# Transformer layer pair in fp32 on one core: the first attention's scores from stacked high and low parts, and an earlier start of the first norm's squares

## The reference, cut to what matters

```python
def forgetting_attention(q, k, v, log_f):
    # q, k, v: (B, S, H, 64); log_f: log forget gates
    c = jnp.cumsum(log_f, axis=1)
    ...
        s = jnp.einsum('bqhd,bkhd->bhqk', q_i, k) * 64 ** -0.5
        bias = c_i[..., :, None] - c_keys[..., None, :]
        mask = k_pos[None, :] <= q_pos[:, None]
        s = jnp.where(mask, s + bias, NEG_INF)
        p = jax.nn.softmax(s, axis=-1)
        return jnp.einsum('bhqk,bkhd->bqhd', p, v)

xn = rms_norm(h, norm_mix_g)
qa, ka, va, fa, cq, ckv, kr, ga, gb = jnp.split(xn @ w_in, splits)
ya = forgetting_attention(qa, ka, va, log_sigmoid(fa + b_forget))
yb = latent_attention(...)       # 8 heads, query and key of 64 + 32 features
merged = sigmoid(ga) * (ya @ w_branch_a) + sigmoid(gb) * (yb @ w_branch_b)
```

## Time and profile before

| | us |
|---|---|
| median of 3 runs (lowest, highest) | 2146.44 (2146.40, 2148.82) |
| the profiled execution, its own time | 2147.04 |
| its span, from the first to the last instruction | 2145.2 |
| busy: PE, its weight loads, DVE, ACT, POOL | 2110.5, 1784.4, 1324.4, 1007.1, 701.9 |
| mean granted TensorE clock | 0.993 |
| first attention, from head 0's first transpose to head 7's end | 123.2 to 215.1 |

### The profile page before, as it was taken

How to read it: one execution, slowest core, us unless ns; L and a number is a source line. 1 busy time by engine, 2 the same in 40 slices (tenths; PEclk the granted TensorE clock), 3 DMA queues, 4 the chain that set the end, 5 groups by cost and what they waited for, 6 DMA issues and landing times.

```text
span 2145.2 us, 31345 instructions
## 1 busy us (share of the span) xinstructions
PE 2110.5 (98%) x10842; PEld 1784.4 (83%) x10842; DVE 1324.4 (62%) x2182; ACT 1007.1 (47%) x1771; POOL 701.9 (33%) x523
## 2 busy tenths in 40 slices
PE   8999999999999999999999999999999999999998
PEld 6878888888888888898887788888877888888886
DVE  5467774466762276775268788788768336676523
ACT  4345664543442253444234567777646325334322
POOL 2011345323233261443327701211155415133331
PEclk9999999999999999999999999999999999999998
DMA  5211235334433333443234322222264533434321
GB/s 171 79 47 67 84 112 190 101 122 153 150 124 108 98 108 113 161 138 123 94 101 156 118 69 75 79 75 79 94 202 138 185 99 118 135 132 167 104 93 65
DMA packets 73423, 248.15 MB, mean 116 GB/s; under 512 B 8080, under 2 KB 8336, under 8 KB 72944
## 3 DMA queue, kind: packets, MB, share of 16 engines
q1 hardware_dynamic: 51120, 182.08, 26.0%
q0 software_dynamic: 10496, 37.56, 5.1%
q10 hardware_dynamic: 11712, 27.27, 3.5%
HBM read 227.48 MB, written 18.87 MB: 115 GB/s over the span
## 4 chain that ended last, share of the span: by engine, by line
PE 83%; DVE 8%; ACT 2%; POOL 2%; issue 2%; DMA 1%; DVEq 0%; POOLq 0%; SPq 0%; ACTq 0%
PE bank L188 24%; PE bank L190 24%; PE bank L189 24%; PE bank L194 3%; PE bank L195 3%; POOL hid L738 2%; PE bank L2128 2%; DVE w_lo L162 1%; DMA w_raw<-stream 1%; DVE gn_r L2730 1%; PE bank L912 1%; DVE xn_lo L608 1%; ACT w_hi L157 1%; DVE h L622 1%; POOL hid L1471 1%
## 5 line engine op out<-in xcount | busy, mean ns | idle before, releaser
L162 DVE TENSOR_TENSOR w_lo<-w_raw,w_hi 128x1024 fp32r<-128x1024 f32 x337 | 454.8, 1353 | 425.1 <-ACT w_hi L157 422.2
L188 PE MATMUL bank<-xn_hi,w_hi 128*128 128x512 f32 (+1 forms) x1432 | 554.7, 387 | 4.1 <-DVE w_lo L162 2.6
L157 ACT ACTIVATE w_hi<-w_raw 128x1024 fp32r<-128x1024 f32 x337 | 354.7, 1054 | 414.0 <-PE bank L190 248.2
L189 PE MATMUL bank<-xn_lo,w_hi 128*128 128x512 f32 (+1 forms) x1432 | 539.1, 376 | 0.0
L190 PE MATMUL bank<-xn_hi,w_lo 128*128 128x512 f32 (+1 forms) x1432 | 538.8, 376 | 0.0
L188 PEld LDWEIGHTS bank<-xn_hi,w_hi 128*128 128x128 f32 x1432 | 271.1, 189 | 56.6 <-DVE h L622 5.2
L190 PEld LDWEIGHTS bank<-xn_hi,w_lo 128*128 128x128 f32 x1432 | 269.8, 188 | 50.2
L189 PEld LDWEIGHTS bank<-xn_lo,w_hi 128*128 128x128 f32 x1432 | 271.0, 189 | 45.7 <-issue 2.9
L188 PE MATMUL bank<-down_hi,w_hi 128*128 128x512 f32 x528 | 205.8, 390 | 0.0
L190 PE MATMUL bank<-down_hi,w_lo 128*128 128x512 f32 x528 | 205.4, 389 | 0.0
L189 PE MATMUL bank<-down_lo,w_hi 128*128 128x512 f32 x528 | 205.4, 389 | 0.0
(11 more groups left out here) (462 smaller groups left out, 4272.7 us busy)
## 6 DMA issues: line engine op xcount, KB each, us to landing
w_raw<-stream SPq DMA_DIRECT2D x337, 512.0 KB, 3.5
s_raw<-stream POOLq DMA_DIRECT2D x48, 512.0 KB, 6.3
spill_g<-gate_out ACTq DMA_DIRECT2D x16, 256.0 KB, 2.0
m_more<-spill_g POOLq DMA_DIRECT2D x3, 1024.0 KB, 12.5
x<-xt SPq DMA_DIRECT2D x4, 512.0 KB, 7.1
x<-xt ACTq DMA_DIRECT2D x1, 2048.0 KB, 9.3
spill_x<-x ACTq DMA_DIRECT2D x1, 2048.0 KB, 6.5
spill_ga<-ga_out ACTq DMA_DIRECT2D x8, 256.0 KB, 2.1
```

The costliest lines, as they stand in the source:

```text
L157: nc.scalar.activation(w_hi[:, slot, :], w_raw[:, slot % 2, :], ACT.Copy).then_inc(split_hi, 1)
L162: nc.vector.tensor_tensor(w_lo[:, slot, :], w_raw[:, slot % 2, :], w_hi[:, slot, :], ALU.subtract).then_inc(split_lo, 1)
L188: nc.tensor.matmul(to, a_hi, b_hi, start=start, stop=False, skip_group_check=True)
L189: nc.tensor.matmul(to, a_hi, b_lo, start=False, stop=False, skip_group_check=True)
```

## The change

Three things are done.

First, a head's operands are stacked. `q_both` holds the head's query in its high part on the head's own 64 partitions and in its low part on the other 64. `k_own` (two tiles, for even and odd heads) holds the key's high part on the head's own 64 partitions and zeros, set once, on the others. `k_mixed` holds the key's low part on the own 64 and its high part on the others. `q_both` against `k_own` and against `k_mixed`, both on 128 partitions, add up to the three products of before. The triangle product stays. [...] 

Second, head 0's scores are made within the last chunk of V instead of after it, and head 1 is staged ahead of the V staging.

Third, ACT squares tiles 0 to 3 of x ahead of the third chunk's high part, and the fourth chunk's high part comes after the square of tile 5 instead of tile 3.

The diff, with its unchanged lines cut:

```diff
@@ -823,6 +823,9 @@
         ks_hi = sb("ks_hi", [P, S], F32R, W0 + 2 * T2)
...
         vs = sb("vs", [P, TB, 2, P], F32R, W0 + 4 * T2)
+        q_both, k_mixed, k_own = qs_hi, ks_lo, (ks_hi, qs_lo)
+        q_rest = sb("q_rest", [P, S], F32R, 54 * K)
+        crossed = sem("att_crossed")
         prob = sb("prob", [P, 2, OFF[TB]], F32, W0 + 6 * T2)
...
         pt_lo = sb("pt_lo", [P, OFF[TB]], F32R, W0 + 27 * K)
@@ -884,7 +887,7 @@
 
...
             s, z = att_sems, dict(atts)
-            for k, n in dict(staged_hi=16 if latent else 8, staged_lo=16 if latent else 8, v_hi=4, v_lo=4, scored=32,
+            for k, n in dict(staged_hi=16 if latent else 24, staged_lo=16, v_hi=4, v_lo=4, scored=32,
                              biased=32, negated=8, exp=32, inverse=8, scaled=32, turned=32, hi=32, lo=32, summed=32, half=8, out=8,
...
                 atts[k] += n
@@ -892,13 +895,17 @@
             gate0 = 8 if latent else 0
...
             def score(pe, h):
-                r = slice(0, P) if latent else slice(64 * (h % 2), 64 * (h % 2) + 64)
-                pe.wait_ge(s["staged_lo"], 2 * (h + 1 if latent else h // 2 + 1) + z["staged_lo"])
+                pe.wait_ge(s["staged_lo"], 2 * (h + 1) + z["staged_lo"])
+                if not latent:
+                    pe.wait_ge(s["staged_hi"], 3 * (h + 1) + z["staged_hi"])
+                    pe.wait_ge(crossed, 16 * (h + 1))
                 for place_of, qb in enumerate(SCORE_ORDER):
...
                     at, n = slice(qb * P, (qb + 1) * P), (qb + 1) * P
-                    last = mm3(score_bank(qb), qs_hi[r, at], qs_lo[r, at], ks_hi[r, 0:n], ks_lo[r, 0:n], True, latent)
-                    if not latent:
+                    if latent:
+                        last = mm3(score_bank(qb), qs_hi[:, at], qs_lo[:, at], ks_hi[:, 0:n], ks_lo[:, 0:n])
+                    else:
+                        mm2(score_bank(qb), q_both[:, at], k_own[h % 2][:, 0:n], k_mixed[:, 0:n], True, False)
                         last = nc.tensor.matmul(score_bank(qb)[:, qb * P:n], ident_r[:], tri_r[:], start=False,
...
                     last.then_inc(s["scored"], 1)
@@ -945,22 +952,37 @@
 
...
 
-                tile = h if latent else h // 2
                 at_least(act, s["scored"], 4 * h, z["scored"])
-                nc.scalar.activation(qs_hi[:], q_raw[:, tile, :], ACT.Copy).then_inc(s["staged_hi"], 1)
-                nc.scalar.activation(ks_hi[krows, :], k_raw[krows, tile, :], ACT.Copy).then_inc(s["staged_hi"], 1)
+                if latent:
+                    nc.scalar.activation(qs_hi[:], q_raw[:, h, :], ACT.Copy).then_inc(s["staged_hi"], 1)
+                    nc.scalar.activation(ks_hi[krows, :], k_raw[krows, h, :], ACT.Copy).then_inc(s["staged_hi"], 1)
+                    return
+                r, other = halves(h % 2)
+                nc.scalar.activation(q_both[r, :], q_raw[r, h // 2, :], ACT.Copy).then_inc(s["staged_hi"], 1)
+                nc.scalar.activation(k_own[h % 2][r, :], k_raw[r, h // 2, :], ACT.Copy).then_inc(s["staged_hi"], 1)
+                nc.scalar.activation(k_mixed[other, :], k_raw[r, h // 2, :], ACT.Copy).then_inc(s["staged_hi"], 1)
 
             def stage_low(pool, h):
-                tile = h if latent else h // 2
-                pool.wait_ge(s["staged_hi"], 2 * tile + 1 + z["staged_hi"])
-                nc.gpsimd.tensor_tensor(qs_lo[:], q_raw[:, tile, :], qs_hi[:], ALU.subtract).then_inc(s["staged_lo"], 1)
-                pool.wait_ge(s["staged_hi"], 2 * tile + 2 + z["staged_hi"])
                 if latent:
-                    pool.wait_ge(s["staged_lo"], 2 * tile + 1 + z["staged_lo"])
-                nc.gpsimd.tensor_tensor(ks_lo[krows, :], k_raw[krows, tile, :], ks_hi[krows, :],
-                                        ALU.subtract).then_inc(s["staged_lo"], 1)
-                if latent:
-                    pool.wait_ge(s["staged_lo"], 2 * tile + 2 + z["staged_lo"])
+                    pool.wait_ge(s["staged_hi"], 2 * h + 1 + z["staged_hi"])
+                    nc.gpsimd.tensor_tensor(qs_lo[:], q_raw[:, h, :], qs_hi[:], ALU.subtract).then_inc(s["staged_lo"], 1)
+                    pool.wait_ge(s["staged_hi"], 2 * h + 2 + z["staged_hi"])
+                    pool.wait_ge(s["staged_lo"], 2 * h + 1 + z["staged_lo"])
+                    nc.gpsimd.tensor_tensor(ks_lo[krows, :], k_raw[krows, h, :], ks_hi[krows, :],
+                                            ALU.subtract).then_inc(s["staged_lo"], 1)
+                    pool.wait_ge(s["staged_lo"], 2 * h + 2 + z["staged_lo"])
+                    return
+                r, other = halves(h % 2)
+                pool.wait_ge(s["staged_hi"], 3 * h + 1 + z["staged_hi"])
+                at_least(pool, crossed, 16 * h)
+                nc.gpsimd.tensor_tensor(q_rest[r, :], q_raw[r, h // 2, :], q_both[r, :], ALU.subtract
+                                        ).then_inc(s["staged_lo"], 1)
+                pool.wait_ge(s["staged_lo"], 2 * h + 1 + z["staged_lo"])
+                pool.dma_start(q_both[other, :], q_rest[r, :]).then_inc(crossed, 16)
+                pool.wait_ge(s["staged_hi"], 3 * h + 2 + z["staged_hi"])
+                nc.gpsimd.tensor_tensor(k_mixed[r, :], k_raw[r, h // 2, :], k_own[h % 2][r, :], ALU.subtract
+                                        ).then_inc(s["staged_lo"], 1)
+                pool.wait_ge(s["staged_lo"], 2 * h + 2 + z["staged_lo"])
 
...
                 return v_raw[:, :, i * P:(i + 1) * P].rearrange("p t (j d) -> p t j d", j=2)
@@ -1002,7 +1024,7 @@
 
...
                     highs(h, (0, 1))
-                    if h + 2 < HEADS1 and (latent or h % 2 == 0):
+                    if h + 2 < HEADS1:
                         stage(act, h + 2)
...
                         output(act, h - 1)
@@ -1068,10 +1090,12 @@
 
...
                 for h in range(HEADS1):
-                    if h + 2 < HEADS1 and (latent or h % 2 == 0):
+                    if h + 2 < HEADS1:
                         stage_low(pool, h + 2)
...
                         stage_v_low(pool, h // 2)
+                        if not latent:
+                            pool.wait_ge(s["v_lo"], h // 2 + 1 + z["v_lo"])
                     between(pool, h)
...
             return (z, score, units_pe, stage, stage_low, stage_v, stage_v_low, exps, units_act, biased, scaled, units_dve,
@@ -1145,6 +1169,11 @@
                 for j in range(4):
...
                     for t in range(2):
+                        if j == 3 and t == 1:
+                            pe.wait_ge(m["root"], b["root"] + 2)
+                            pe.wait_ge(a["negc"], 1)
+                            pe.wait_ge(s["mask"], 4)
+                            a_score(pe, 0)
                         k, w = 2 * j + t, slice(t * S, (t + 1) * S)
...
                             at = slice(tb * P, (tb + 1) * P)
@@ -1168,10 +1197,6 @@
                         pe.wait_ge(a["fk"], 1)
...
                         cumulated(1)
-                pe.wait_ge(m["root"], b["root"] + 2)
-                pe.wait_ge(a["negc"], 1)
-                pe.wait_ge(s["mask"], 2)
-                a_score(pe, 0)
                 pe.wait_ge(a["negc"], 2)
...
                 for h in range(3, 7):
@@ -1232,10 +1257,9 @@
                         act.wait_ge(x_in[k // 2], 16)
...
                                          scale=col[:, COLS["mix1"] + k:COLS["mix1"] + k + 1]).then_inc(m["hi"], 1)
-                ahead(high_part, act, fq, 0)
                 for k in range(KT):
-                    if k == 4:
-                        ahead(high_part, act, fq, 1)
+                    if k in (4, 6):
+                        ahead(high_part, act, fq, k // 2 - 2)
                     if k >= 4:
...
                     nc.scalar.activation(squares[:, k % 4, :], x[:, k, :], ACT.Square).then_inc(m["squared"], 1)
@@ -1263,6 +1287,7 @@
                 act.wait_ge(a["rope"], 10)
...
                 act.wait_ge(a["qk"], 8)
+                act.wait_ge(s["mask"], 2)
                 a_stage(act, 0)
...
                 nc.scalar.activation(lft_hi[:], banks[3][:, 0:32], ACT.Copy).then_inc(a["lft_hi"], 1)
@@ -1282,6 +1307,7 @@
                 negated(0)
...
                 ahead(high_part, act, fv, 3)
+                a_stage(act, 1)
                 act.wait_ge(a["v"], 4)
...
                 for h in range(2, 5):
@@ -1446,7 +1472,7 @@
                     nc.vector.tensor_tensor(mq[:, n, :], banks[n if n < 4 else n - 1][:], rope_c[:], ALU.mult
...
 
-                dve.wait_ge(s["mask"], 3)
+                dve.wait_ge(s["mask"], 5)
                 for n in range(4):
...
                 ahead(low_part, dve, fu, 0)
@@ -1473,14 +1499,17 @@
                 pool.wait_ge(m["added"], nb["added"] + KT - 1)
...
                 nc.gpsimd.tensor_copy(cumul[:], cumul_raw[:]).then_inc(consts_made, 1)
+                for tile in k_own:
+                    nc.gpsimd.memset(tile[:].bitcast(F32), 0.0).then_inc(s["mask"], 1)
```

(6 more changed lines are left out.)

## The result

The changed kernel takes 2131.12 us in the median of four runs (2129.91 to 2133.74), the kernel before in the same set 2147.63 us; the ratio is 0.9927, 95% interval [0.9913, 0.9941]. It is faster by 16.5 us in the medians, where 16.2 were forecast. A second set of five runs gave 0.9944 [0.9930, 0.9957] (2132.89 against 2144.71, 11.8 us), so the gain is 12 to 16 us, with the forecast at its upper end. The execution profiled here was the slowest of its four: 2133.74 us about a span of 2132.1.

The account below looks back on a forecast made before the run. The matmul engine, at 98% of the span, was taken as the bound. Savings of 4.7 up to head 0, 10.4 in heads 0 to 5 and 1.1 for squares, 16.2 us, gave about 2130.2 us; range 2128 to 2133, chance 0.60.

Parts of the forecast that it names:

- The sum: Whole kernel: 4.7 up to head 0, 10.4 in heads 0 to 5, 1.1 for squares, together 16.2 us saved.
- Bound: Whole kernel: PE fills 98% of the span, so only time taken off PE or waits put onto it move the end.
- The score: First attention, per head: scores fall from 3.58 to 1.75 us, with weight loads hidden; loads in the open had chance 0.03.
- Up to head 0: From V's last product to head 0: starts near 118.5 instead of 123.23, 4.7 us gained, despite a 0.5 us wait.
- The transfer: Query's crossing, heads 0 to 5: 1.0 us of waits, range 0 to 5; transfer making the kernel slower had chance 0.05.
- New waits in heads 2 to 4: PE waits for DVE's late remainder pt_lo: 2.7, 1.9 and 0.4 us plus smaller holds, together 5.6, bounds 3 and 8.
- The forecast's last term: Head 4: DVE's chain once more, with 2.0 us of scalings for the 3.3 us reciprocal, makes PE wait 0.4 us.
- POOL beside DVE: Heads 2 to 4: upper bound of 8 us on the new waits, each a us longer from POOL working beside DVE.
- Low clock: Up to head 5: half-filled array costs 8.4 us; all but 1.7 goes. Low clock staying had chance 0.17.
- Heads 6 and 7: End of the first attention: these heads score nothing and stay at 15.79 us.
- Heads 0 to 5 in all: First attention: 57.4 us plus 5.6 waits, 1.0 transfer, 1.7 clock gives 65.7 against 76.1, a gain of 10.4.
- Squares: Start of the kernel: PE's 1.13 us wait for POOL's sum of squares goes, a gain of 1.1 us.

Follow-up runs that it names:

- The late transfer: Changed kernel with the transfer of the query's low part issued behind POOL's second subtraction, 1.36 us later: 2135.42 us, ratio 0.9953.
- the repeat: The changed kernel run and profiled once more, with nothing altered, in a second set: 2132.89 us, ratio 0.9944.
- the early reciprocals: Changed kernel with DVE's two reciprocals moved from heads 1 and 2 to ahead of V's copy out of its banks: 2130.08 us, ratio 0.9928.
- the squares alone: Kernel before with only the order of ACT's squares and third and fourth chunks changed: 2143.98 us, ratio 0.9990.
- the scores alone: Changed kernel with ACT's squares put back in the order of the kernel before: 2133.03 us, ratio 0.9945.

## Why the prediction was right, and where it was not

- **The sum.** 16.2 us forecast; 16.5 and 11.8 by the medians of two sets, 13.1 and 17.6 by the spans of two profiles. That the first comes within 0.3 us is luck: terms missed by 1 to 2 us in both directions, and executions of one kernel differ by more.
- **Bound.** Right: time taken off PE's scores came back as time of the kernel.
- **The score.** 1.75 forecast, 1.67 measured; the loads are hidden.
- **Up to head 0.** 4.7 forecast, 4.5 measured, with the wait for the third copy of the gates at 0.72 us instead of 0.5.
- **The transfer.** 1.0 us was set aside, none was paid: it lands after 2.2 us, not 3.0. The late transfer shows that the slack is 0.3 to 0.5 us, so landing 0.8 us later, at the 3.0 us of the earlier trace rows, it would have cost some heads 0.3 to 0.5 us each.
- **New waits in heads 2 to 4.** 5.6 forecast; 4.03 + 1.23 + 0.56 = 5.8 measured, and 2.92 + 1.25 + 0.56 = 4.7 in the repeat. The forecast's last term, 0.4 for head 4, comes to 0.6 by its own working (4.8 + 6.4 + 2.0 + 1.8 + 0.6 = 15.6, less head 3's 11.5, is 4.1 into head 4, where PE asks at 3.5). The mechanism and the place are confirmed by the early reciprocals. The size in head 2 was off by 1.3 us in this profile, 1.1 of it DVE's small product behind POOL. The forecast had "POOL beside DVE" only as a bound, a microsecond each time.
- **Low clock.** The step that failed is "I take the half-filled array as the cause". Half-row scores without row changes ran at 1.00. That the time came out all the same is luck: the change removes the row changes too. The 8.4 us that were to go are also one execution's, as the 3.4 of the kernel with the squares alone show; by the mean clocks of all executions (0.993 before, 0.996 in the nine of the changed kernel) the clock gave back some 0.0025 x 2145 = 5 us, an estimate. The forecast let 1.7 us of low clock remain, "in head 2 or 3, where PE will stand idle"; it stood there, from 142 to 150, at 0.57: 0.43 x 8 = 3.4 us, behind the 4.03 us wait, and 1.7 in the repeat.
- **Heads 6 and 7.** Forecast unchanged; they lost 1.6 us, 1.3 of it head 6's wait for the same held product. Nothing had been looked for there because these heads score nothing; but it is head 6 in which POOL makes V's low part beside DVE's maxima.
- **Heads 0 to 5 in all.** 10.4 forecast, 11.0 measured in the repeat and 9.1 in this profile: -1.7 (clock), -0.2 (waits), +1.0 (transfer), and 0.4 from heads that end in the low clock or are a little over 9.56.
- **Squares.** 1.1 forecast; the wait of 1.13 is gone. The profile has 2.4 us less up to the cumulated gate, the repeat 1.5, and all 13 profiles 1.5 in the mean. The times with the squares alone can't tell these apart (0.2 to 4.1).

## What to carry to other kernels

Count products on the matmul engine by their rows too: a short product whose rows differ from its neighbours' costs a quarter of a microsecond, and parts of a stream full of these ran at half clock with the engine busy all the time. After a stage has been made shorter, look down the list of everything else that sits between two uses of its slowest helper, for it was hidden by the time removed: here edits worth 1 us before were worth 8 to 11 after it. And among those, look for tiny instructions of DVE beside GpSimd's long ones. A ledger by stages of one profile should be laid beside that of a second execution before its terms are read to a microsecond.

## What the runs showed of the hardware

- A DVE product of 128x4 numbers took 0.17 us alone and 1.25, 1.26, 1.28 and 1.64 us when a GpSimd subtraction (1.27 us) had begun 0.02 us or more before it, or, for the last, in the middle of GpSimd's issue of a transfer with a subtraction behind it. Begun 0.08 to 0.10 us into such an issue it took 0.17, three times. Starting at the same hundredth of a microsecond as a subtraction it was not held (142.10 and 175.09 in the repeat); 0.01 us behind one it was held in one case (1.27 us, at 143.16 in the kernel with the scores alone) and not in another (0.17, at 176.15 in the changed kernel).
- In these kernels TensorE's clock was at its lower level after each idle time of 2.05, 2.92, 2.99, 3.18 and 4.03 us in the first attention, and not after those of 1.85, 1.37 or less. The two waits of 2.99 us were followed by 1.7 and by 3.4 us lost (0.86 in 140 to 152 us, 0.76 in 138 to 152). In the kernel before it fell without any idle time, where products alternate between 64 and 128 rows (0.92 from 116 to 204 us). From V's last product on that lost 8.4 us in one execution, and 3.4 in one of the kernel with the squares alone, whose scores are the same.
- A lone product of 128 rows between products of 64 cost 0.27 us beyond one of 64 (scores of 3.58 and 2.51 us, four such products each); weight loads of 0.19 us ran beside products on the same 128 rows.
- An ACT copy from 64 partitions to the other 64 (64x512) took 0.63 us.
- Eight transfers of 64 partitions x 2 KB across the partitions landed 2.2 us after the issue each time, where four of the same shape in the kernel before took 2.5 to 3.7.
